# First layers of four gated feed-forwards by a seven-product scheme, with weight sums on GpSimd

## The chip, the cores and the metric

The kernel runs on one core of a Trainium2 chip. The metric is the device time of one execution in microseconds (us). TensorE (PE in the profile) multiplies; VectorE (DVE), ScalarE (ACT) and GpSimd (POOL) work element by element; SyncE (SP) issues the loads.

## What is computed

Two models of width 1024 run one after the other over 512 tokens, all in float32. The first has one block of dilated, stick-breaking and memory attention and a gated feed-forward with a short convolution. The second has two layers, one with a gated block mixer and one with a recurrent mixer (RWKV-7). Each of the two layers has two gated feed-forwards, so there are four of them, called 00, 01, 10 and 11, and they are what is changed:

```python
def swiglu(x, w13, w2):
    gate, up = jnp.split(x @ w13, 2, axis=-1)      # w13: 1024 x 5632, w2: 2816 x 1024
    return (jax.nn.silu(gate) * up) @ w2
```

The input `x` of each is a root-mean-square norm of the residual stream.

## The kernel before

Activations lie transposed in SBUF: a tile is 128 features by 512 tokens, and x has 8 tiles (`KD`). To keep float32's accuracy, every operand of a product is split in a high part (rounded to the fp32r type, a CAST on ScalarE) and a low part (the rest, a subtraction on VectorE), and each product is three matmuls: high by high, high by low, low by high. So `xh`, `xl` are the two parts of x and `wh`, `wl` those of a chunk of weights.

**Weights.** They come in a fixed stream of chunks (`STREAM`, `order`). SyncE loads chunk n into one of two slots of `raw` (128 x 2048, 1 MB) as soon as chunk n-2 has its low part (`lo_ready`). `split_hi` (ScalarE, L320) and `split_lo` (VectorE, L336) split it. `chunks_used` counts the chunks that TensorE has finished.

**The first layer of a feed-forward** is a `linear` stage of 22 units (`KF`), named up_00 and so on. A unit is one chunk: 8 tiles of x by two blocks of 128 output features, one of the gate and one of the value. It issues 8 x 2 x 3 = 48 matmuls (L518) with a moving operand of 128x512, into two banks of PSUM, in turn of two groups of banks. For each unit `swiglu` has VectorE scale both outputs by the norm's factor `rs` (L2443, L2444), ScalarE apply Silu (L2435), VectorE multiply (L2448), ScalarE make the high part `hid_h` (L2424) and VectorE the low part `hid_l` (L2428).

**The norm runs late.** x enters the products with its gain alone; the factor 1/rms is applied to the outputs. `Deferred` (L987) makes `xh` (ScalarE, L1047) and `xl` (VectorE, L1100) tile by tile while the products of units 0 and 1 start. Where a post-norm precedes it, GpSimd adds the tiles to the residual stream (`add_on_pool`, L921). After that, ScalarE squares (L767) and VectorE adds seven times (L859), TensorE sums over partitions (`sum_pe`, L802) inside unit 1, ScalarE takes the root (`square_root`, L776), VectorE inverts and makes a diagonal (L868 to L872), and TensorE spreads it (`spread_pe`, L843) inside unit 2. TensorE stands still wherever one of these is not ready.

**The second layer** (down_00 and so on) has 8 units of two chunks of 1408 columns (`halves`); a unit is 22 tiles by 3 matmuls in one bank. Its first unit waits for each tile of the hidden activations (`norms=Made`, L650), which are all split by then except the last.

Everything is written by hand: each engine has its own list of instructions, with waits on semaphores. An engine never passes a waiting instruction.

## Time and profile before

| | before |
|---|---|
| median of 3 runs | 3256.67 us (3254.47 to 3256.72) |
| profiled execution, first to last instruction | 3256.1 us |
| what lies around it: median less this span | 0.6 us |
| TensorE busy | 3198.5 us (98%), 20322 matmuls |
| VectorE busy | 1772.9 us (54%) |
| ScalarE busy | 1250.6 us (38%) |
| GpSimd busy | 136.1 us (4%), 134 instructions |
| granted TensorE clock | 0.997 of full speed, mean |
| DMA queues | 88 GB/s, 24.7% of 16 engines for the weights |

The profile is one execution. Its page gives busy times, the chain of work that ended last, and groups of instructions; the trace gives single instructions with their start. A row of a matmul shows its whole latency, and the matmuls overlap: the pace is read from the distance of starts.

### The profile page before, as it was taken

The numbers are of one execution on the slowest core, as the hardware profiler recorded it, in microseconds if no ns is written. First come the engines' busy times: TensorE is split into PE (matmuls) and PEld (weight loads), VectorE is DVE, ScalarE is ACT, GpSimd is POOL, SyncE is SP. The second block draws the span as 40 slices with busy tenths as digits, with TensorE's granted clock in tenths as the row PEclk, the third lists the DMA queues.
The fourth block names the chain that finished last, engine by engine and source line by source line (L and its number), as shares of the span: only waits on it lengthen the run. The fifth ranks groups of instructions, "written<-read, shape, count | busy, mean of one in ns | idle before, by whom it ended". The sixth has DMA issues, their size and how long they took to land.

```text
span 3256.1 us, 46645 instructions
## 1 busy us (share of the span) xinstructions
PE 3198.5 (98%) x20322; PEld 2628.9 (81%) x20322; DVE 1772.9 (54%) x2127; ACT 1250.6 (38%) x1605; POOL 136.1 (4%) x134
## 2 busy tenths in 40 slices
PE   9999999999999999999999999999999999999998
PEld 7887787888788888987888887888777777788886
DVE  6456766774454435463644357444666656654437
ACT  3357544443232223442422244223336554332224
POOL 2100000000000001000100011000120000100001
PEclk9999999999999999999999999999999999999999
DMA  5211222222232223222222222222222000232231
GB/s 194 99 53 65 104 91 91 92 103 89 92 104 91 89 96 126 91 78 97 91 99 83 98 99 88 95 95 89 84 80 101 16 4 15 84 104 91 88 106 65
DMA packets 47211, 286.68 MB, mean 88 GB/s; under 512 B 6416, under 2 KB 6688, under 8 KB 21408
## 3 DMA queue, kind: packets, MB, share of 16 engines
q1 hardware_dynamic: 44960, 279.51, 24.7%
q0 software_dynamic: 2048, 4.20, 0.4%
q8 instruction: 160, 2.62, 0.3%
q14 instruction: 43, 0.35, 0.0%
HBM read 277.39 MB, written 2.10 MB: 86 GB/s over the span
## 4 chain that ended last, share of the span: by engine, by line
PE 80%; DVE 5%; ACT 2%; issue 1%; POOL 0%; DVEq 0%; ACTq 0%
PE ps L518 70%; PE ps L3700 3%; PE ps L3738 1%; PE ps L1242 1%; DVE wl L336 1%; ACT wh L320 1%; PE ps L1243 1%; PE ps L1244 1%; DVE xl L3174 0%; PE ps L2790 0%; PE ps L985 0%; DVE tmp L3182 0%; DVE conv L2473 0%; PE ps L3745 0%; PE ps L3777 0%
## 5 line engine op out<-in xcount | busy, mean ns | idle before, releaser
L518 PE MATMUL ps<-xh,wh 128*128 128x512 f32 (+1 forms) x2464 | 966.1, 392 | 13.1 <-DVE xl L3174 3.4
L518 PE MATMUL ps<-xl,wh 128*128 128x512 f32 (+1 forms) x2464 | 941.9, 390 | 3.3 <-POOL xl L3071 3.0
L518 PE MATMUL ps<-xh,wl 128*128 128x512 f32 (+1 forms) x2464 | 910.3, 391 | 0.3 <-DVE wl L336 0.3
L336 DVE TENSOR_TENSOR wl<-raw,wh 128x2048 fp32r<-128x2048 f32 (+2 forms) x283 | 590.4, 2086 | 424.0 <-ACT wh L320 423.7
L320 ACT CAST wh<-raw 128x2048 fp32r<-128x2048 f32 (+1 forms) x280 | 485.9, 1735 | 283.7 <-PE ps L518 275.4
L518 PEld LDWEIGHTS ps<-xh,wh 128*128 128x128 f32 (+1 forms) x2464 | 462.4, 188 | 122.3 <-issue 18.7
L518 PEld LDWEIGHTS ps<-xl,wh 128*128 128x128 f32 (+1 forms) x2464 | 461.7, 188 | 105.1 <-POOL xl L3071 3.8
L518 PEld LDWEIGHTS ps<-xh,wl 128*128 128x128 f32 (+1 forms) x2464 | 461.8, 188 | 99.4 <-issue 1.0
L518 PE MATMUL ps<-hid_h,wh 128*128 128x512 f32 x880 | 342.9, 390 | 1.2 <-DVE wl L336 1.2
L518 PE MATMUL ps<-hid_l,wh 128*128 128x512 f32 x880 | 342.4, 389 | 0.0
L518 PE MATMUL ps<-hid_h,wl 128*128 128x512 f32 x880 | 342.4, 389 | 0.0
L2435 ACT ACTIVATE tmp<-tmp 128x512 f32<-128x512 f32 x88 | 55.8, 634 | 539.4 <-DVE tmp L2443 539.3
L2443 DVE TENSOR_TENSOR tmp<-ps,rs 128x512 f32<-128x512 f32 x88 | 60.8, 691 | 292.7 <-PE ps L518 287.5
L518 PEld LDWEIGHTS ps<-hid_h,wh 128*128 128x128 f32 x880 | 165.2, 188 | 37.0 <-DVE wl L336 3.1
L518 PEld LDWEIGHTS ps<-hid_l,wh 128*128 128x128 f32 x880 | 165.2, 188 | 34.4
L518 PEld LDWEIGHTS ps<-hid_h,wl 128*128 128x128 f32 x880 | 165.2, 188 | 34.2
L921 POOL TENSOR_TENSOR h<-tmp,h 128x512 f32<-128x512 f32 x42 | 66.5, 1612 | 2610.4 <-DVE tmp L914 2610.4
L1293 DVE COPY ybuf<-ps 128x512 f32<-128x512 f32 x40 | 27.7, 692 | 179.6 <-PE ps L518 156.7
L2428 DVE TENSOR_TENSOR hid_l<-tmp,hid_h 128x512 fp32r<-128x512 f32 x110 | 76.2, 693 | 77.1 <-ACT hid_h L2424 77.1
L1337 ACT ACTIVATE tmp<-ybuf 128x512 f32<-128x512 f32 x35 | 22.1, 632 | 246.7 <-DVE ybuf L1293 192.4
L2424 ACT CAST hid_h<-tmp 128x512 fp32r<-128x512 f32 x110 | 68.3, 621 | 86.6 <-DVE tmp L2448 67.0
L518 PE MATMUL ps<-wh,xh 128*128 128x256 f32 x352 | 94.7, 284 | 0.1
(494 smaller groups left out, 4017.7 us busy)
## 6 DMA issues: line engine op xcount, KB each, us to landing
raw<-in_up SPq DMA_DIRECT2D x88, 1024.0 KB, 4.7
raw<-in_down SPq DMA_DIRECT2D x64, 704.0 KB, 4.1
raw<-in_up_c SPq DMA_DIRECT2D x22, 1024.0 KB, 4.7
raw<-in_down_c SPq DMA_DIRECT2D x16, 704.0 KB, 4.0
raw<-in_gates SPq DMA_DIRECT2D x8, 1024.0 KB, 4.7
raw<-in_gv SPq DMA_DIRECT2D x8, 1024.0 KB, 4.8
raw<-in_gu SPq DMA_DIRECT2D x8, 1024.0 KB, 4.7
raw<-in_gout SPq DMA_DIRECT2D x8, 1024.0 KB, 4.7
```

The lines of the kernel that those rows point to most:

```text
L320: nc.scalar.copy(wh[:, slot, 0:w], raw[:, slot, 0:w]).then_inc(hi_ready, 1)
L336: nc.vector.tensor_tensor(wl[:, slot, 0:w], raw[:, slot, 0:w], wh[:, slot, 0:w].bitcast(F32), ALU.subtract).then_inc(lo_ready, 1)
L518: last = nc.tensor.matmul(out, stationary, moving, start=(fresh and q == 0), stop=(t == kt - 1 and half == per - 1 and q == 2), skip_group ...
L921: nc.gpsimd.tensor_tensor(dst, self.scratch(2 + t % 2), dst, ALU.add).then_inc(n_onto.sem, 1)
L1242: nc.tensor.matmul(ps[:, b, :], wh[0:r, slot, wc], hi[0:r], start=(t == 0), stop=False, skip_group_check=True)
L1243: nc.tensor.matmul(ps[:, b, :], wh[0:r, slot, wc], lo[0:r], start=False, stop=False, skip_group_check=True)
L1244: last = nc.tensor.matmul(ps[:, b, :], wl[0:r, slot, wc], hi[0:r], start=False, stop=(t == self.kt - 1), skip_group_check=True)
L2424: nc.scalar.copy(hid_h[:, k, tokens], tmp[:, 2 + u, tokens]).then_inc(act_steps.sem, 1)
L2428: nc.vector.tensor_tensor(hid_l[:, k, tokens], tmp[:, 2 + u, tokens], hid_h[:, k, tokens].bitcast(F32), ALU.subtract).then_inc(dve_steps.s ...
L2435: nc.scalar.activation(tmp[:, u, :], tmp[:, u, :], ACT.Silu).then_inc(act_steps.sem, 1)
L2443: nc.vector.tensor_tensor(tmp[:, u, :], products[0], rs[:, :], ALU.mult).then_inc(dve_steps.sem, 1)
L3700: last = nc.tensor.matmul(out(e, c), left(lhs, e, c), right(rhs, e, c), start=(n == 0), stop=(n == len(pairs) - 1), skip_group_check=True)
```

## The change

Each of the four first layers is now a class of its own, `SwigluUp`, in place of a `linear` stage with `swiglu`.

- Units 0 to 2 (`PLAIN`) are multiplied as before. Units 3 to 21 (19 of 22) go by Strassen's scheme in Winograd's form. The products of a unit form a 2 x 2 block matrix of weights (even or odd tiles of x, gate or value) by a 2 x 2 block matrix of x (even or odd tiles, first or last 256 tokens). Seven block products take the place of eight. Each is 4 pairs of tiles by 3 matmuls with a moving operand of 128x256: 84 matmuls for 48.
- **Terms of x**, once a stage: four combinations for each pair of tiles (`terms`), 16 instructions of 128x256 on VectorE and four on ScalarE, then four CASTs of 128x1024 on ScalarE for their high parts, and their low parts by two subtractions of 128x1024 on VectorE and two on GpSimd.
- **Sums of weights**, for each of the 19 units: GpSimd makes S1 to S4, four instructions of 128x512 (`sums_of`). It starts those of unit u when TensorE has finished unit u-2. Splitting a chunk is now a CAST and a subtraction of 128x1536 (three plain blocks) and two of each of 128x1024 (the sums).
- **Outputs**: ScalarE copies the first product (128x256), VectorE does seven additions of 128x256 that each read one product from PSUM, scales gate and value in one instruction of 128x1024, and multiplies.
- **The split of the hidden activations** is moved out of the units to the end of the stage: 11 CASTs of 128x1024 on ScalarE and 11 subtractions, 8 on VectorE and 3 on GpSimd (`POOL_PAIRS`). The high parts lie where the terms and `xl` were, so the last unit runs pair by pair of tiles to free them.
- The chunks' columns are laid out by quarters, for the convolutional feed-forward too, whose instructions stay as they are. The embedding's split moves from unit 5 of the first layer to unit 2 of the second.

The diff, cut to its core:

```diff
+        def evict(self, dve, unit):
...
+            dve.wait_ge(u_copied.sem, u_copied.after(k, 1))
+            dve.wait_ge(chunks_used, self.a + unit + 3)
+            nc.vector.tensor_tensor(v1, g1, r[5], ALU.add).then_inc(u_added.sem, 1)
...
+        def sums_of(self, pool, unit):
+            n, k, x = self.a + unit, unit - PLAIN, self.slot(unit)
+            pool.wait_ge(raw_ready[n % 2], 16 * (n // 2 + 1))
+            pool.wait_ge(chunks_used, n + 1 if unit > PLAIN else self.a + 3)
...
+            nc.gpsimd.tensor_tensor(s1, a21, a22, ALU.add).then_inc(w_sum.sem, 1)
+            nc.gpsimd.tensor_tensor(s3, a11, a21, ALU.subtract).then_inc(w_sum.sem, 1)
+            pool.wait_ge(chunks_used, n + 1)
+            pool.wait_ge(w_sum.sem, w_sum.after(k, 1))
+            nc.gpsimd.tensor_tensor(s2, s1, a11, ALU.subtract).then_inc(w_sum.sem, 1)
+            pool.wait_ge(w_sum.sem, w_sum.after(k, 3))
+            nc.gpsimd.tensor_tensor(s4, a12, s2, ALU.subtract).then_inc(w_sum.sem, 1)
...
+        def gpsimd(self):
...
+                for j in range(2):
+                    self.term_low(pool, nc.gpsimd, pool_low, j)
+                for unit in range(PLAIN, KF):
+                    self.sums_of(pool, unit)
+                for p in self.POOL_PAIRS:
+                    self.hidden_low(pool, nc.gpsimd, pool_low, p)
...
+        def scalar(self):
...
+                norm.squares_act(act)
+                self.term_high(act, 0)
+                self.term_high(act, 1)
+                n = a + 2
+                split_hi(act, n, 16 * (n // 2 + 1), n % 2, order[n][2])
+                self.term_high(act, 2)
+                self.term_high(act, 3)
+                self.plain_high(act, 3)
+                norm.scale_act(act)
...
+        def vector(self):
...
+                split_lo(dve, a + 1, (a + 1) % 2, order[a + 1][2])
+                self.terms_of(dve, 0)
+                norm.squares_dve(dve)
+                self.terms_of(dve, 2)
+                norm.scale_dve(dve)
+                split_lo(dve, a + 2, a % 2, order[a + 2][2])
...
+                for unit in range(PLAIN, KF - 2):
+                    self.evict(dve, unit)
+                    self.scale(dve, unit)
+                    self.plain_low(dve, unit + 2)
+                    self.hide(dve, unit)
+                    self.sum_low(dve, unit + 2, 0)
+                    self.sum_low(dve, unit + 2, 1)
...
+        def quad_waits(self, pe, unit, i):
+            if i == 0:
+                pe.wait_ge(psum_read.sem, self.read + (1 if unit == PLAIN else unit - 1))
+                pe.wait_ge(w_low.sem, w_low.after(unit - PLAIN, 1))
...
+            if i == 3:
+                pe.wait_ge(w_low.sem, w_low.after(unit - PLAIN, 2))
...
+            if i == 5:
+                pe.wait_ge(lo_ready, self.a + unit + 1)
...
-        linear(f"up_{layer}{n}", KD, 256, x_split, norms=norm, between=between, paired="filled", **swiglu(norm))
-        linear(f"down_{layer}{n}", HALF, P, hid_split, halves=True, norms=Made(lambda t: 4 * t + 4),
-               **(sums or summing(ybuf, 1)))
+        up = SwigluUp(f"up_{layer}{n}", norm)
+        linear(f"down_{layer}{n}", HALF, P, up.split, halves=True, second_ahead=True, norms=up,
+               between=embedding(layer) if embeds else {}, **(sums or summing(ybuf, 1)))
```

How it moves instructions. First VectorE at the start of stage 00, after the last `xl`; before:

```order
L336 TENSOR_TENSOR wl_52<-raw_50,wh_51 128x2048
L859 TENSOR_TENSOR rs_56<-rs_56,tmp_57 128x512 x7
L868 TENSOR_SCALAR stats_59<-ps 128x4
L870 RECIPROCAL stats_59<-stats_59 128x4
L872 TENSOR_TENSOR rs_56<-const_58,stats_59 128x512
```

and with the change:

```order
L344 TENSOR_TENSOR wl_52<-raw_50,wh_51 128x2048
L2722 SCALAR_TENSOR_TENSOR terms_4771<-h_53,vec_49,terms_4771 128x256 x4
L2732 SCALAR_TENSOR_TENSOR terms_4771<-h_53,vec_49,terms_4771 128x256 x2
L2722 SCALAR_TENSOR_TENSOR terms_4771<-h_53,vec_49,terms_4771 128x256 x2
L868 TENSOR_TENSOR rs_56<-rs_56,tmp_57 128x512 x7
L2722 SCALAR_TENSOR_TENSOR terms_4771<-h_53,vec_49,terms_4771 128x256 x4
L2732 SCALAR_TENSOR_TENSOR terms_4771<-h_53,vec_49,terms_4771 128x256 x2
L2722 SCALAR_TENSOR_TENSOR terms_4771<-h_53,vec_49,terms_4771 128x256 x2
L877 TENSOR_SCALAR stats_59<-ps 128x4
L879 RECIPROCAL stats_59<-stats_59 128x4
```

Eight instructions for the terms now stand ahead of the norm's seven adds, and eight between them and the norm's inverse.

VectorE in one unit of the middle of a stage, before:

```order
L336 TENSOR_TENSOR wl_52<-raw_50,wh_51 128x2048
L2443 TENSOR_TENSOR tmp_57<-ps,rs_56 128x512
L2444 TENSOR_TENSOR tmp_57<-ps,rs_56 128x512
L2448 TENSOR_TENSOR tmp_57<-tmp_57 128x512
L2428 TENSOR_TENSOR hid_l_4767<-tmp_57,hid_h_4766 128x512
```

and with the change:

```order
L2695 TENSOR_TENSOR tmp_57<-tmp_57,ps 128x256
L2696 TENSOR_TENSOR tmp_57<-tmp_57,ps 128x256
L2698 TENSOR_TENSOR tmp_57<-tmp_57,ps 128x256
L2700 TENSOR_TENSOR tmp_57<-tmp_57,ps 128x256
L2702 TENSOR_TENSOR tmp_57<-tmp_57,ps 128x256
L2703 TENSOR_TENSOR tmp_57<-tmp_57,ps 128x256
L2705 TENSOR_TENSOR tmp_57<-tmp_57,ps 128x256
L2710 TENSOR_TENSOR tmp_57<-tmp_57,rs_56 128x1024
L2663 TENSOR_TENSOR plain_l_7506<-raw_50,plain_h_7505 128x1536
L2715 TENSOR_TENSOR hid_4768<-tmp_57 128x512
L2673 TENSOR_TENSOR sums_l_7509<-sums_7507,sums_h_7504 128x1024
L2673 TENSOR_TENSOR sums_l_7510<-sums_7508,sums_h_7504 128x1024
```

Five instructions became twelve. GpSimd had none in the units; it now has, at the start of a stage:

```order
L2645 TENSOR_TENSOR terms_l_4772<-terms_4771,terms_h_4770 128x1024 x2
L2635 TENSOR_TENSOR sums_7507<-raw_50 128x512
L2636 TENSOR_TENSOR sums_7507<-raw_50 128x512
L2639 TENSOR_TENSOR sums_7508<-sums_7507,raw_50 128x512
L2641 TENSOR_TENSOR sums_7508<-raw_50,sums_7508 128x512
```

The last four rows stand 19 times in each stage.

## Rows read from the trace of the kernel before

**Rows 1.** The page: busy times, and the chain that ended last by engine and line.

```profile
PE 3198.5 (98%) x20322; PEld 2628.9 (81%) x20322; DVE 1772.9 (54%) x2127; ACT 1250.6 (38%) x1605; POOL 136.1 (4%) x134
...
PE 80%; DVE 5%; ACT 2%; issue 1%; POOL 0%; DVEq 0%; ACTq 0%
```

**Rows 2.** Chain in order of time, stages 00 and 01: start us, us, what.

```profile
906.73 0.79 PE ps L802 x8
...
910.85 0.86 PE ps L843 x2
911.71 335.28 PE ps L518 x1478
...
1276.31 0.79 PE ps L802 x8
...
1280.56 0.86 PE ps L843 x2
```

**Rows 3.** TensorE by time, matmuls of 256 columns: start us, us, engine, line.

```profile
1339.80 0.28 PE L518 MATMUL ps<-wl,xh 128*128 128x256 f32 x1
...
1347.84 0.28 PE L518 MATMUL ps<-wh,xl 128*128 128x256 f32 x1
```

**Rows 4.** VectorE by time, part of one unit of stage 00.

```profile
942.16 0.69 DVE L2443 TENSOR_TENSOR tmp<-ps,rs 128x512 f32<-128x512 f32 x1 [3.94 <-PE ps L518]
942.77 0.68 DVE L2444 TENSOR_TENSOR tmp<-ps,rs 128x512 f32<-128x512 f32 x1
```

**Rows 5.** Busy time in a stretch of stage 00: PE, PEld, DVE, ACT, POOL, clock, DMA share.

```profile
930.00:1120.00 190.00, 190.00 (x840) 157.34 (x839) 87.81 (x90) 54.56 (x55) 0.00 (x0) 1.00 0.27 95
```

**Rows 6.** VectorE: groups by shape with mean ns, and a pair of 256-column instructions.

```profile
L336 DVE TENSOR_TENSOR wl<-raw,wh 128x2048 fp32r<-128x2048 f32 x198 | 455.1, 2298 | 257.8 <-ACT wh L320 257.5 <-DVE vec L1535 0.3
L336 DVE TENSOR_TENSOR wl<-raw,wh 128x1408 fp32r<-128x1408 f32 x80 | 130.0, 1625 | 162.4 <-ACT wh L320 162.4
...
3236.69 0.76 DVE L2614 TENSOR_TENSOR tmp<-ps,rs 128x256 f32<-128x256 f32 x2 [2.73 <-PE ps L518]
```

**Rows 7.** GpSimd and VectorE by time while both work, before stage 01.

```profile
1253.35 1.28 POOL L921 TENSOR_TENSOR h<-tmp,h 128x512 f32<-128x512 f32 x1 [1127.40 <-DVE tmp L914]
...
1253.46 1.72 DVE L1100 SCALAR_TENSOR_TENSOR xl<-h,vec,xh 128x512 fp32r<-128x512 f32 x1 [0.20 <-ACT xh L1047]
...
1259.38 0.73 DVE L914 SCALAR_TENSOR_TENSOR tmp<-ybuf,vec,ps 128x512 f32<-128x512 f32 x1
1260.04 1.13 DVE L1100 SCALAR_TENSOR_TENSOR xl<-h,vec,xh 128x512 fp32r<-128x512 f32 x1
1261.09 0.74 DVE L914 SCALAR_TENSOR_TENSOR tmp<-ybuf,vec,ps 128x512 f32<-128x512 f32 x1
...
1266.59 0.75 DVE L1100 SCALAR_TENSOR_TENSOR xl<-h,vec,xh 128x512 fp32r<-128x512 f32 x1 [0.30 <-ACT xh L1047]
```

**Rows 8.** The same two engines at the recurrent mixer's start, and one GpSimd line's durations.

```profile
2369.15 3.12 DVE L336 TENSOR_TENSOR wl<-raw,wh 128x2048 fp32r<-128x2048 f32 x1
...
2370.08 3.08 POOL L3124 TENSOR_TENSOR dx<-hn 128x511 f32<-128x511 f32 x1
...
L3124 POOL TENSOR_TENSOR dx<-hn x8: 1034/1487/3084, 2367.2 to 2379.2; 128x511 f32<-128x511 f32 x8
```

**Rows 9.** VectorE and ScalarE by time at the start of stages 00 and 01.

```profile
896.75 5.46 DVE L859 TENSOR_TENSOR rs<-rs,tmp 128x512 f32<-128x512 f32 x7
...
908.20 0.69 DVE L872 TENSOR_TENSOR rs<-const,stats 128x512 f32<-128x512 f32 x1
...
1269.46 5.46 DVE L859 TENSOR_TENSOR rs<-rs,tmp 128x512 f32<-128x512 f32 x7
...
903.64 1.91 ACT L320 CAST wh<-raw 128x2048 fp32r<-128x2048 f32 x1 [2.36 <-PE ps L518]
915.88 0.62 ACT L2424 CAST hid_h<-tmp 128x512 fp32r<-128x512 f32 x1 [0.76 <-DVE tmp L2448]
```

**Rows 10.** The page: issues of the chunks of the first layers, KB each, us to landing.

```profile
raw<-in_up SPq DMA_DIRECT2D x88, 1024.0 KB, 4.7
```

399 lines of the change are left out of this document (370 added, 29 removed).

## The prediction

> **What bounds the kernel now.** I read the page first: TensorE is busy for 98% of the span and is 80% of the chain that ended last [rows 1]; the granted clock is 1.00 of full speed, 2.4 GHz, in the stretch used below [rows 5]. Then the chain in order of time: in stage 00, 1478 matmuls follow one another for 335.28 us without a wait, through the rest of the first layer and the second [rows 2]. That is 226.8 ns for one with 512 columns. So only what shortens TensorE's list, or makes it wait, counts; before the change there is no stall at the seam between the layers. Last, busy time in a stretch of the same stage: VectorE works 87.8 of 190 us, ScalarE 54.6, GpSimd not at all [rows 5]. A unit takes 48 x 226.8 ns = 10.89 us, and VectorE has half of it free. The chunk for a unit lands 4.7 us after its issue [rows 10] and is not late in any case below.
>
> **1. TensorE's products.** Matmuls with 256 columns start 120 ns apart: 67 of them lie in the 8.04 us from 1339.80 to 1347.84 [rows 3]. A seven-product unit is 84 x 120 ns = 10.08 us, 0.81 less than 10.89. Over 19 units and four stages that is 61 us saved. The rows are of products with x stationary, here the weights are; the load of the stationary operand has the same form, so I take 120 ns. From 129.6 ns up the gain would be gone (10.89 / 84). The Trainium skill, "TensorE: Matmul & The Clock Gate", section "Back-to-back issue gap", gives N/2.4 + 2.5 ns for a single warm matmul, 109 and 216 ns; by it a unit would gain 1.2 us, this term would be 91 us instead of 61, and the case below in which TensorE sets the pace would end 30 us earlier. The rows here show 120 and 227 ns, so I keep the rows.
>
> **2. VectorE's turn per unit.** Instructions of 512 columns start 0.61 us apart [rows 4]; the two L336 shapes give (2298 - 1625) / 640 = 1.05 ns a column; two of 256 take 0.76 us, so they start 0.34 apart [rows 6]. Hence 1024 columns take 1.15 us and 1536 take 1.68. A turn is seven PSUM additions (7 x 0.34, and some 0.3 for results awaited), scale 1.15, low part of the plain blocks 1.68, multiply 0.61, low parts of the sums 2 x 1.15: 8.4 us. Alone it would fit in 10.08.
>
> **3. But it is not alone: GpSimd.** A sum of 512 columns takes it 1.28 us, and while it runs, a VectorE instruction with two inputs in SBUF stands: L1100 at 1253.46, begun 0.11 us after GpSimd's, takes 1.72 us instead of the 0.75 of the one at 1266.59 [rows 7]. L914, which has one input in PSUM, takes its usual 0.73 beside it. In the steady alternation L914 recurs after 1.71 us, of which VectorE's 512 columns are 0.53, so GpSimd keeps it out for 1.17 [rows 7]. It goes both ways: a GpSimd instruction whose shortest is 1.03 us took 3.08 when it met L336, and L336 took 3.12 instead of 2.30 [rows 8, 6]. When both want the way, they alternate; back-to-back VectorE instructions do not keep GpSimd out (L336 at 2369.15 was let in last). The Trainium skill, "SBUF — State Buffer", section "Who interferes with whom", says that a VectorE instruction with two SBUF inputs contends with a GpSimd instruction that reads SBUF, and that whoever issues first keeps the other out for the whole instruction. By that the hold would be 1.28, the turn worked out below 12.2 us, and the sum 53 us higher. The rows agree on who waits, and show 1.17.
>
> For the sums I take 1.12: the nearest row is L921 (1.17), but S1 and S3 read both inputs from one tile, as L3124 does, whose shortest is 1.03 (a hold of some 0.93) [rows 8]. The ends are 0.93 and 1.28. The seven PSUM additions (2.7 us) are free ground for two sums. The other two each hold VectorE: 8.4 + 2 x 1.12 = 10.6 us, over TensorE's 10.08. So VectorE falls behind by half a microsecond or more a unit. TensorE does not feel it at first: unit u+2 starts on the low part of the plain blocks, which VectorE has after 2.7 + 1.15 + 2.2 (holds) + 1.68 = 7.7 us of its turn, 2.3 us in hand. But GpSimd is released by TensorE's end of a unit, not by VectorE; once VectorE is late, the sums fall on the low-part subtractions of the turn before and only one lies beside the additions. Then three are paid: 8.4 + 3 x 1.12 = 11.8 us; I take 11.7. With five of the 19 units at 10.08 and 14 at 11.7: 14 x 1.62 = 22.7 us a stage, **+91 us** in all. Ends: nothing (hold 0.93 to 1.08, never late), and 17 x 2.1 = 36 us a stage (hold 1.28, late at once).
>
> **4. The start of a stage.** In 00, VectorE began its seven adds at 896.75 and took 5.46 [rows 9]. Eight term instructions (0.40 each, 0.34 and a scalar operand's 0.06) go ahead: adds end at 905.4, before TensorE's sum at 906.73 [rows 2]. In 01 the adds end at 1269.46 + 3.2 + 5.5 = 1278.1, and the sum was at 1276.31: 1.8 us late. Then eight more term instructions, 3.2 us alone, with both inputs in SBUF. Beside them GpSimd now has two low parts of 1024 columns (twice 1.17, estimate 2.3 each) and four sums, 9 us, and each can hold one short term instruction: +8 (0 to 9), so they end at 905.4 + 11.2 = 916.6. ScalarE stands behind them with two CASTs of 1024 columns and one of 1536 ahead of the root. From 0.62 and 1.91 us for 512 and 2048 columns [rows 9] the last of these and the root add 2.5: 919.1. Inverse and diagonal about 1 (the diagonal alone 0.69 [rows 9]), spread 0.86 [rows 2]: 921.0 for 911.71, **9.3 us**. In 01 the adds end 3.0 us later relative to the spread (1278.1 against 1280.56, 905.4 against 910.85): 12.3. The other two stages have a post-norm too, I count them as 01. Sum 9.3 + 3 x 12.3 = **+46 us**. Without any hold the term instructions would end at 908.6, the three CASTs and the root at 912.1 and the spread at 914.0, 2.3 us late, and 5.3 in the others: 18, since the CASTs ahead of the root remain. That is the low end; with 9 us of holds the high end is 50.
>
> **5. The seam.** The hidden activations are split at the end. After the products of unit 20 VectorE has: additions and scale 3.9, split of a chunk 1.6 (1408 columns [rows 6]), five low parts 5.8, another chunk 1.6, additions and scale of unit 21 3.9, two low parts and two multiplies 3.5, a wait for ScalarE's last CAST 1.0 and the last low part 1.2: 22.5 us. GpSimd's three low parts of 1024 columns hold it for up to 6.9 more: 29. TensorE wants the last pair 10.08 + 15.0 - 1.4 = 23.7 us after unit 20. So it waits 5 to 8 (VectorE starts late, by 3): I take 7.5, **+30 us** in all; bounds 2 (no hold) and 9 a stage. The rest of the second layer has little VectorE work, the embedding's split, moved there, is hidden by it, and would cost its few microseconds if it were not. The x tiles' copies by quarters change addresses alone: 0.
>
> **Sum**, against the execution profiled (3256.1, 0.6 under the median): -61 + 91 + 46 + 30 = +106 us, or 3363 with the 0.6.
>
> **Rivals.**
> - *Units stay at TensorE's pace.* Start and seam are held as above, but the sums are short like L3124 and VectorE never falls behind (decides: hold under 1.08 us). -61 + 46 + 4 x 6.5 = +11: 3268. For it: two of four sums have both inputs in one tile. Against: L921 at 1253.35, with nothing in its way, took 1.28 [rows 7]; and L3124's inputs lie one element apart, which the sums' don't.
> - *Faster: the holds hardly bite.* GpSimd is released just when VectorE begins its additions from PSUM, which rows show undelayed; if GpSimd then runs beside additions and ScalarE's waits only, TensorE sets the pace, with 18 us for the starts and 8 for the seams: -61 + 18 + 8 = -35: 3222. It decides where fewer than two sums a unit and none of the term instructions are held. Against it: the rows show a hold at every meeting.
> - *The half-width products don't run at 120 ns.* At 135 ns a unit is 11.3 us: +34 us from TensorE instead of -61; beside a VectorE at 11.7 it adds nothing, beside a free one it gives about 3257 + 34 + 26 = 3317.
>
> **How the numbers follow.** Forecast 0.60, units at TensorE's pace 0.18, faster 0.17, slow products 0.05. Time 3363. The range reaches down to the faster case, 3218, and up to 3390, which takes in a hold of 1.17 (11.9 us a turn, 15 units late, +17 us) and 10 us more at starts and seams; a hold of 1.28 (3416) and the best of the faster cases are left out, some 0.15 together. A run of this kernel can tell 0.2%, 6.5 us. The faster case and the short end of the second make 0.20 for faster; 3268 with its bounds gives 0.07 within 0.2%; the rest, 0.73, is slower. The likeliest case's own range is 3335 to 3390.
>
> **What would show it.** Right: GpSimd's L2635 to L2641 well over 1.28 us each; VectorE's L2663 and L2673 at a mean over 0.6 us above 1.76 and 1.22; TensorE's ends of units 10.1 us apart at first and 11.7 later, idle in front of the first product of a unit, released by VectorE's L2663; a wait of 9 us or more at L843; one of some 7 us in the second layer's first unit. Wrong: 84 matmuls every 10.1 us to the end of a stage, or GpSimd's sums at 1.0 us, or a short wait at L843.

## The result, and the profile after

| | before | after |
|---|---|---|
| median | 3256.3 us (4 runs) | 3326.2 us (3319.9 to 3329.8, 4 runs) |
| ratio | | 1.0212 [1.0198, 1.0227] |
| profiled execution, span | 3256.1 us | 3328.0 us |
| TensorE, VectorE, GpSimd busy | 98%, 54%, 4% | 96%, 69%, 22% |
| mean granted clock | 0.997 | 0.986 |

Slower by 70 us (2.1%), where 106 were forecast. The execution that was profiled is the slowest of the four and lies 3.6 us above their median, so the profile accounts for 71.9 us and not 70. The page of the changed kernel, which answers to [rows 1]:

```profile
PE 3179.5 (96%) x23058; PEld 2724.9 (82%) x23058; DVE 2303.2 (69%) x2739; ACT 1401.7 (42%) x1821; POOL 723.7 (22%) x458
```

TensorE has less to do and waits more. The way to see where the time went is one instruction that stands once at the head of every stage: VectorE's reciprocal of the norm after the previous part. In the following lines "the reciprocal" is always this one. Its rows, of the kernel before and then of the changed one:

```profile
881.81 0.95 DVE L864 RECIPROCAL rs<-rs 128x128 f32<-128x128 f32 x1 [1.85 <-ACT rs L772]
1248.97 0.95 DVE L864 RECIPROCAL rs<-rs 128x128 f32<-128x128 f32 x1 [0.58 <-ACT rs L772]
1539.53 0.95 DVE L864 RECIPROCAL rs<-rs 128x128 f32<-128x128 f32 x1 [0.58 <-ACT rs L772]
1908.70 0.95 DVE L864 RECIPROCAL rs<-rs 128x128 f32<-128x128 f32 x1 [1.16 <-ACT rs L772]
```

```profile
882.43 0.95 DVE L873 RECIPROCAL rs<-rs 128x128 f32<-128x128 f32 x1 [1.85 <-ACT rs L781]
1271.06 0.95 DVE L873 RECIPROCAL rs<-rs 128x128 f32<-128x128 f32 x1 [0.58 <-ACT rs L781]
1561.60 0.95 DVE L873 RECIPROCAL rs<-rs 128x128 f32<-128x128 f32 x1 [0.58 <-ACT rs L781]
1946.37 0.95 DVE L873 RECIPROCAL rs<-rs 128x128 f32<-128x128 f32 x1 [1.16 <-ACT rs L781]
```

Stage 00 is the first interval, the mixer between is the second, stage 01 the third: 367.16 and 388.63 us; 290.56 and 290.54; 369.17 and 384.77. Read in the same way, stage 10 went from 369.95 to 386.23 and 11 from 369.49 to 385.60. So 21.5, 15.6, 16.3 and 16.1 us, 69.5 of the 71.9 by which the spans differ, and nothing elsewhere but 2.4. Inside a stage there are three places, and TensorE's idle time shows them. Start of stages 00 and 01:

```profile
921.56 2.08 PE L852 MATMUL ps<-rs,const 128*128 128x512 f32 x2 [10.10 <-DVE rs L881]
...
1606.26 2.08 PE L852 MATMUL ps<-rs,const 128*128 128x512 f32 x2 [8.05 <-DVE rs L881]
```

Then the units by halves (3 to 21, whose products are 256 tokens wide): TensorE's wait in front of a unit's first product is 0.21 us in stage 01, but 1.3 in the second half of stage 00.

```profile
1059.32 0.36 PE L2825 MATMUL ps<-xh,plain_h 128*128 128x256 f32 x1 [1.30 <-DVE plain_l L2663]
1070.93 0.36 PE L2825 MATMUL ps<-xh,plain_h 128*128 128x256 f32 x1 [1.31 <-DVE plain_l L2663]
...
1709.06 0.36 PE L2825 MATMUL ps<-xh,plain_h 128*128 128x256 f32 x1 [0.21 <-DVE plain_l L2663]
1719.58 0.35 PE L2825 MATMUL ps<-xh,plain_h 128*128 128x256 f32 x1 [0.21 <-DVE plain_l L2663]
```

A unit takes 11.61 us in stage 00 and 10.52 in stage 01. TensorE's units are not late at once: in each stage the first seven by halves start 10.08 us apart. And the seam between the two layers, six waits of 6.9 us together in stage 01 (five are shown):

```profile
1819.83 0.50 PE L527 MATMUL ps<-terms_h,wh 128*128 128x512 f32 x1 [0.69 <-DVE hid_r L2533]
...
1825.86 0.50 PE L527 MATMUL ps<-xl,wh 128*128 128x512 f32 x1 [1.71 <-DVE wl L344]
1830.76 0.50 PE L527 MATMUL ps<-xl,wh 128*128 128x512 f32 x1 [1.23 <-DVE hid_r L2533]
1835.45 0.50 PE L527 MATMUL ps<-terms_l,wh 128*128 128x512 f32 x1 [1.29 <-DVE last_hid_r L2533]
1838.79 0.47 PE L527 MATMUL ps<-terms_h,wh 128*128 128x512 f32 x1 [1.67 <-DVE wl L344]
```

Added up by TensorE's starts against the reciprocal: starts +13.0, +16.2, +16.9 and +17.1 (63), lateness in the units 14 and three times 5 (29), seams 9.7 each (39), elsewhere 2.4, and -61.4 for products of 120 ns. That is 72. Of each seam's 9.7 us some 2.3 are handed on by the late units: with no unit late, in runs 1 and 4, the rest of a stage behind the start of its last unit is shorter by that. Late units therefore cost 29 + 4 x 2.3, some 38 us in all.

**Why two rhythms.** One turn of VectorE and GpSimd in stage 01, and one in stage 00:

```profile
1728.20 1.75 DVE L2663 TENSOR_TENSOR plain_l<-raw,plain_h 128x1536 fp32r<-128x1536 f32 x1
1729.87 0.69 DVE L2715 TENSOR_TENSOR hid<-tmp 128x512 f32<-128x512 f32 x1
1730.47 4.56 DVE L2673 TENSOR_TENSOR sums_l<-sums,sums_h 128x1024 fp32r<-128x1024 f32 x2
...
1730.03 1.68 POOL L2635 TENSOR_TENSOR sums<-raw 128x512 f32<-128x512 f32 x1 [3.00 <-PE ps L2827]
1731.67 2.27 POOL L2636 TENSOR_TENSOR sums<-raw 128x512 f32<-128x512 f32 x1
1733.90 2.28 POOL L2639 TENSOR_TENSOR sums<-sums,raw 128x512 f32<-128x512 f32 x1
1736.26 1.30 POOL L2641 TENSOR_TENSOR sums<-raw,sums 128x512 f32<-128x512 f32 x1
...
1092.24 1.75 DVE L2663 TENSOR_TENSOR plain_l<-raw,plain_h 128x1536 fp32r<-128x1536 f32 x1
1093.91 1.78 DVE L2715 TENSOR_TENSOR hid<-tmp 128x512 f32<-128x512 f32 x1
1095.62 4.54 DVE L2673 TENSOR_TENSOR sums_l<-sums,sums_h 128x1024 fp32r<-128x1024 f32 x2
...
1093.44 1.71 POOL L2635 TENSOR_TENSOR sums<-raw 128x512 f32<-128x512 f32 x1 [3.72 <-DMA raw<-in_up]
1095.11 1.75 POOL L2636 TENSOR_TENSOR sums<-raw 128x512 f32<-128x512 f32 x1
```

The pair L2673 alone takes 2.35 us, L2715 0.68. When a VectorE instruction has to stand while one of GpSimd's runs, I call that a hold. A hold costs VectorE (4.56 - 2.35) / 2 = 1.10 us. In these rows the two engines alternate, one of GpSimd's sums to one of VectorE's instructions: what counts is not how many sums there are but how many VectorE instructions with both inputs in SBUF stand between the first sum and the additions from PSUM. In stage 01 the sums begin just behind the start of L2715 and hold two; in stage 00 they begin while L2663 still runs, hold three, and the turn is 1.1 us longer. In stage 00 they are released by the chunk's landing, 5 us after VectorE's turn began and its load was issued; in 01 by TensorE's end of a unit, 5.6 us after. Each rhythm keeps itself up, as these rows suggest: what releases the sums is itself timed by VectorE's or TensorE's last turn.

### The profile page after: what moved, and what is told of

It reads as the page before. It is cut to its first block and busy times, and to the rows that moved or that the text cites. A ratio compares the mean times of both kernels' runs of the same rounds, so it can differ in the third digit from the quotient of the medians.

```text
span 3328.0 us, 53477 instructions
## 1 busy us (share of the span) xinstructions
PE 3179.5 (96%) x23058; PEld 2724.9 (82%) x23058; DVE 2303.2 (69%) x2739; ACT 1401.7 (42%) x1821; POOL 723.7 (22%) x458
## 5 line engine op out<-in xcount | busy, mean ns | idle before, releaser
L344 DVE TENSOR_TENSOR wl<-raw,wh 128x2048 fp32r<-128x2048 f32 (+1 forms) x207 | 415.9, 2009 | 330.6 <-ACT wh L328 330.3
L527 PE MATMUL ps<-xl,wh 128*128 128x512 f32 x1248 | 479.9, 392 | 14.5 <-DVE wl L344 7.7
L328 ACT CAST wh<-raw 128x2048 fp32r<-128x2048 f32 (+2 forms) x204 | 340.9, 1671 | 273.5 <-PE ps L527 264.7
L527 PE MATMUL ps<-xh,wh 128*128 128x512 f32 x1056 | 416.2, 394 | 14.5 <-DVE xl L1109 4.0
L527 PE MATMUL ps<-xh,wl 128*128 128x512 f32 x1056 | 390.1, 392 | 0.3 <-DVE wl L344 0.3
L527 PEld LDWEIGHTS ps<-xl,wh 128*128 128x128 f32 x1248 | 233.4, 187 | 69.5 <-DVE wl L344 9.9
L2673 DVE TENSOR_TENSOR sums_l<-sums,sums_h 128x1024 fp32r<-128x1024 f32 x152 | 285.1, 1910 | 0.1
L2825 PE MATMUL ps<-terms_h,sums_h 128*128 128x256 f32 x912 | 259.3, 284 | 2.0 <-DVE sums_l L2673 2.0
L2826 PE MATMUL ps<-terms_l,sums_h 128*128 128x256 f32 x912 | 258.5, 283 | 0.0
L2827 PE MATMUL ps<-terms_h,sums_l 128*128 128x256 f32 x912 | 258.5, 283 | 0.0
L527 PE MATMUL ps<-hid_r,wh 128*128 128x512 f32 x640 | 250.8, 392 | 0.0
```

Source lines behind the costliest of these rows:

```text
L328: nc.scalar.copy(wh[:, slot, 0:w], raw[:, slot, 0:w]).then_inc(hi_ready, 1)
L344: nc.vector.tensor_tensor(wl[:, slot, 0:w], raw[:, slot, 0:w], wh[:, slot, 0:w].bitcast(F32), ALU.subtract).then_inc(lo_ready, 1)
L527: last = nc.tensor.matmul(out, stationary, moving, start=(fresh and q == 0), stop=(t == kt - 1 and half == per - 1 and q == 2), skip_group ...
L2673: nc.vector.tensor_tensor(x.sums_l[part][:, :, :], x.sums[part][:, :, :], x.sums_h[:, 2 * part:2 * part + 2, :].bitcast(F32), ALU.subtract ...
L2825: nc.tensor.matmul(out, high, moving, start=(j == 0 and i % 2 == 0), stop=False, skip_group_check=True)
L2826: nc.tensor.matmul(out, high, moving_low, start=False, stop=False, skip_group_check=True)
```

## The experiments

Each ran on the chip beside the kernel before, whose median was 3255.8 to 3257.0 us, so 1 or 2 us between two runs say nothing. Gains are against the changed kernel's 3326.2. Lengths of single stages are read from the reciprocal's rows of one profiled execution each.

**1. No weight sums.**

```
-            nc.gpsimd.tensor_tensor(s1, a21, a22, ALU.add)
+            nc.gpsimd.tensor_tensor(s1[:, 0:1], a21[:, 0:1], a22[:, 0:1], ALU.add)
```

and so for s3, s2 and s4; sum_high and sum_low read the raw quarters instead of the sums. So this kernel leaves out the sums of the weights.

> GpSimd's four instructions of a weight sum are cut from 512 columns to 1, and ScalarE and VectorE split the raw quarters in place of the sums, with instructions of the same size; so this kernel leaves out the summing of the weights. Theory A (a GpSimd sum keeps a VectorE instruction with two SBUF inputs waiting about 1.10 us; three stages pay two holds a unit and run at 10.51 us, stage 00 pays three and runs at 11.6): without sums every unit of all four stages takes 10.08 us, the second-half splits take 1.22 us each in place of a mean of 1.91, the 29 us of late units vanish, and each start loses four holds of 1.1 us ahead of VectorE's root work, another 18 us at most: 3326 - 29 - 18 = 3279, between 3275 and 3297. Theory B (VectorE's own list of 8.4 us and ScalarE's order make the units late, the holds fall into VectorE's free time): the pace of the units stays at 10.5 and 11.6 us, only the starts gain: 3308 to 3326.

Measured: 3274.0 us, 52 less. VectorE's group of the sums' splits:

```profile
L2677 DVE TENSOR_TENSOR sums_l<-raw,sums_h 128x1024 fp32r<-128x1024 f32 x152 | 179.2, 1219 | 0.0
```

In the changed kernel its mean was 1910 ns. VectorE's first additions stand 10.08 us apart in all four stages from the second unit by halves to the last but one, so theory A holds for the units. By the stages' lengths that is worth 37 us, with what late units hand on to the seam. The starts got 4 us shorter each (stage 01's first unit by halves ends 62.1 us after the reciprocal in place of 66.4), and keep some 9 to 13 us which are not the sums' doing. Theory B falls: VectorE's own list fits.

**2. TensorE kept busy while it waits.**

```
                     if n == 5:
+                        for _ in range(16):
+                            nc.tensor.matmul(ps[:, 3, 0:2 * P], table("ident"), const[:, 0:2 * P], start=True, stop=True)
                         norm.spread_pe(pe)
```

> TensorE computes 16 matmuls of 128x256 on a constant in the stretch in which it waits for the scale ahead of the spread (L852), and is idle there no more. Theory C (beside the 8 to 10 us of the wait, each start pays for matmuls at half the clock behind it: the spread took 2.08 us where it took 0.86 before): the wait's end stays, the granted clock behind it stays near full, the spread takes 0.86 us again and each start gains 3 us: 3326 - 12 = 3314, between 3308 and 3319. Rival D (the clock's drop falls where TensorE would wait for VectorE anyway, or the starts' 62 us are all wait): no change, 3324 to 3328. If the 16 matmuls outlast the wait, each start loses what sticks out, up to 2 us a stage: 3334.

Measured: 3316.6 us, 9.6 less, near what theory C gave, but mostly not for its reason. The granted clock (the number behind the five engines' busy times) around the wait in stage 00, changed kernel and this one:

```profile
911.00:921.00 10.00, 0.46 (x3) 0.03 (x1) 6.90 (x9) 3.47 (x4) 5.70 (x5) 0.63 0.00 0
921.00:935.00 14.00, 13.44 (x50) 10.43 (x51) 13.28 (x12) 5.83 (x7) 0.86 (x1) 0.78 0.31 94
```

```profile
911.00:921.00 10.00, 6.77 (x31) 5.55 (x30) 6.89 (x9) 3.47 (x4) 4.73 (x4) 1.00 0.00 0
921.00:935.00 14.00, 14.00 (x81) 12.12 (x80) 14.00 (x11) 7.20 (x8) 4.49 (x3) 1.00 0.29 92
...
920.58 1.13 PE L852 MATMUL ps<-rs,const 128*128 128x512 f32 x2 [3.23 <-DVE rs L881]
```

In the changed kernel the clock is 0.50 of full speed, 1.2 GHz, in every 2 us from 915 to 927, so for 6 us of products too. That drop goes, and the spread takes 1.13 us in place of 2.08. TensorE's first product by halves starts 2.6 us earlier in stage 00, 1.7 in 01, 2.5 and 2.6 in 10 and 11, which is the clock's price at the start. But VectorE, which then sets the pace, takes part of it back: that unit's products are added up only 2.2 us earlier in stage 00, 1.0 in 01, 1.8 in 11, and stages 01, 10 and 11 end up 0.9, 1.5 and 1.7 us shorter. Stage 00 is 9.3 shorter, since with another phase it fell out of its slow rhythm: its last units take 10.52 us. So the clock costs 1.7 to 2.6 us where it is low and 1 to 2 us at the end of a stage, not 3, and that the total agrees is luck. (The stages' gains add up to more than 9.6, because this run's profiled execution is its fastest and the changed kernel's its slowest.) A total alone would have confirmed the wrong price.

**3. Squares and root first, the terms' low halves on VectorE.**

VectorE, then ScalarE; GpSimd's two term_low go, and VectorE takes all four.

```
                 split_lo(dve, a + 1, (a + 1) % 2, order[a + 1][2])
-                self.terms_of(dve, 0)
                 norm.squares_dve(dve)
-                self.terms_of(dve, 2)
+                self.terms_of(dve, 0)
                 norm.scale_dve(dve)
                 split_lo(dve, a + 2, a % 2, order[a + 2][2])
-                for j in (2, 3):
-                    self.term_low(dve, nc.vector, t_made, j)
+                self.terms_of(dve, 2)
                 self.plain_low(dve, 3)
-                self.sum_low(dve, 3, 0)
                 self.evict_plain(dve, 0)
+                for j in range(KPAIRS):
+                    self.term_low(dve, nc.vector, t_made, j)
+                self.sum_low(dve, 3, 0)
...
                 norm.squares_act(act)
-                self.term_high(act, 0)
-                self.term_high(act, 1)
                 n = a + 2
                 split_hi(act, n, 16 * (n // 2 + 1), n % 2, order[n][2])
-                self.term_high(act, 2)
-                self.term_high(act, 3)
-                self.plain_high(act, 3)
-                norm.scale_act(act)
+                norm.two.square_root(act)
+                self.term_high(act, 0)
+                self.term_high(act, 1)
+                self.plain_high(act, 3)
+                norm.keep_scale(act)
+                self.term_high(act, 2)
+                self.term_high(act, 3)
```

> At the start of each of the four stages the sums of squares come first on VectorE and ScalarE, the first two term pairs next, then the root, and the other two pairs behind it; the low halves of all four terms are taken on VectorE, none on GpSimd. Nothing is left out. Theory A: GpSimd's two low halves (2.5 us each undisturbed) held VectorE's terms for 5 us; with them gone and the root ahead, the wait for the scale at L852 falls from 8.05 and 10.10 us to under 2, the clock stays up, and what is left is lateness of the first unit by halves, which waits for the low halves of the terms, 3 to 6 us a stage: 3326 - 4 x 10 = 3286, between 3276 and 3298. Rival E (the start is bound by the sum of VectorE's work before the first product on halves, not by its order): the wait moves whole from L852 to the first unit by halves, and only the saved holds show, 4 x 2 us: 3318.

Measured: 3294.4 us, 32 less. The wait at L852 is gone in stage 00, and fell only to some 4 us in the other three, not under 2. A further wait, for VectorE to take unit 2 out of PSUM (L2686), took over 2.51 us of it in stage 01; stage 01's first unit by halves ends 59.8 us after the reciprocal (66.4):

```profile
1581.00 2.08 PE L852 MATMUL ps<-rs,const 128*128 128x512 f32 x2 [4.08 <-DVE rs L881]
...
1601.63 0.39 PE L2824 MATMUL ps<-terms_h,sums_h 128*128 128x256 f32 x1 [2.51 <-DVE tmp L2686]
```

6.6, 5.8 and 7.3 us came in stages 01, 10 and 11, and 16.1 in 00, of which 9.5 again are its rhythm. Rival E's 8 us in all is too little. But order and holds were changed in one run, which doesn't part them. What is left of the wait is what GpSimd's four sums, begun at 1571.99, cost the terms: the four term instructions beside them take 5.77 us, the four at 1583.07 take 1.67. Run 7, which starts the sums later, has no such wait.

**4. The scale read from PSUM.**

```
-            nc.vector.tensor_tensor(self.both(unit), self.both(unit), self.spread_scale(), ALU.mult)
+            for b, half in ((3, SOON), (7, LATER)):
+                x = self.both(unit)[:, :, half]
+                nc.vector.tensor_tensor(x, x, ps[:, b, T // 2:T].unsqueeze(1).broadcast_to([P, 2, T // 2]), ALU.mult)
```

ScalarE copies rs there once a stage, behind open(2). The upper halves of these two banks are free, but TensorE writes the other half of such a bank in a unit's seventh product, so it waits there until the scale of the unit before is done.

> The scale of the tokens is copied by ScalarE into two free half banks of PSUM once a stage, and the multiplication of a unit's gate and value by it reads it there, as two instructions of 2x256 columns in place of one of 2x512 that reads SBUF twice; the last two units stay as they were. Nothing is left out. Theory A (only instructions with both inputs in SBUF are held): the instruction that meets the first sum is held no more, VectorE's turn ends inside 10.08 us and most of the 29 us of late units vanish: 3326 - 25 = 3301, between 3295 and 3308. Rival F (the two instructions are longer than one and the next one with two SBUF inputs is held in its place, so the turn stays at 10.5 us): 3322 to 3332.

Measured: 3289.4 us, 37 less. All units of all stages take 10.08 us on average, as without any sums; since the sums are all made here, it was not ScalarE's waiting for them that run 1 took away. Groups of this run's instructions say why:

```profile
L2720 DVE TENSOR_TENSOR tmp<-tmp,ps 128x512 f32<-128x512 f32 x136 | 87.5, 685 | 7.0
L2725 DVE TENSOR_TENSOR hid<-tmp 128x512 f32<-128x512 f32 x80 | 130.1, 1626 | 0.1
L2676 DVE TENSOR_TENSOR sums_l<-sums,sums_h 128x1024 fp32r<-128x1024 f32 x152 | 183.4, 1241 | 0.2
```

With one input in PSUM the scale is never held (685 ns, 512 columns). Three sums pass beside it and the additions, and the fourth, which itself stands while VectorE splits the plain blocks, holds L2725 (1626 ns in place of 685): one hold a unit. VectorE is then faster than TensorE and stays ahead. The Trainium skill, "SBUF — State Buffer", section "Who interferes with whom", says that a VectorE instruction with at most one SBUF input, outside the modes that take two ports, does not contend with GpSimd; these rows agree. The forecast of 25 us was 12 short: it took most of the 29 us of TensorE's late starts, and not the 2.3 us a stage that late units hand on to the seam. Stage 00 is 16.2 us shorter, the others 6 to 8. Rival F falls.

**5 and 6. The seam.** First only the three low halves moved from GpSimd to VectorE:

```
-        POOL_PAIRS = (1, 4, 7)
+        POOL_PAIRS = ()
```

> The three low halves of hidden pairs 1, 4 and 7 that GpSimd takes at the seam of the two layers go to VectorE, in the order of the pairs; nothing else is moved. Theory A (GpSimd's and VectorE's low halves hold each other: VectorE's took 2.69, 3.43 and 3.43 us where an undisturbed one takes 1.21, GpSimd's 8.9 us for three): VectorE does all of them in 1.14 us apiece, is done earlier by 2.69+3.43+3.43-3x1.21 less 3x1.14 = 2.5 us, the second chunk's split and all behind it come 2.5 us earlier, and each seam of 9.7 us gains 1.7 (the 1.71 wait for that split) and up to 1 more of the later waits: 3326 - 4 x 2.2 = 3317. Rival G (the seam's waits come from ScalarE's order, which splits the second chunk behind nine high halves): under 0.5 us a stage, 3324 to 3327.

Measured: 3313.0 us, 13 less; stage 01 is 3.5 us shorter. On VectorE the instructions of L2533, which took 1.23, 2.69, 3.43 and 3.43 us in a row, are now (the group of one form), and TensorE's waits in stage 01's seam are these three alone:

```profile
L2533 DVE TENSOR_TENSOR hid_r<-hid,xl 128x1024 fp32r<-128x1024 f32 x12 | 14.6, 1219 | 0.0
...
1825.20 0.50 PE L527 MATMUL ps<-xl,wh 128*128 128x512 f32 x1 [1.17 <-DVE hid_r L2533]
1829.88 0.50 PE L527 MATMUL ps<-terms_l,wh 128*128 128x512 f32 x1 [1.27 <-DVE last_hid_r L2533]
1833.22 0.47 PE L527 MATMUL ps<-terms_h,wh 128*128 128x512 f32 x1 [1.68 <-DVE wl L344]
```

More than forecast: holds cost more than GpSimd's help was worth. The waits of 0.69, 0.33 and 1.71 us are gone; the last of these was for the second chunk's split, so it was the holds and not ScalarE's order that made that split late. Rival G falls. Then also the order:

ScalarE's part, then VectorE's, where low half 6 to 9 move likewise:

```
-            split_hi(act, n, 16 * (n // 2 + 1), n % 2, order[n][2])
             self.copy_first(act, KF - 1)
-            self.hidden_high(act, HALF - 2)
+            split_hi(act, n, 16 * (n // 2 + 1), n % 2, order[n][2])
+            for p in range(6, HALF - 1):
+                self.hidden_high(act, p)
             self.open(act, KF - 1)
...
-            self.hidden_low(dve, nc.vector, s_low, 6)
             split_lo(dve, n, n % 2, order[n][2])
+            self.hidden_low(dve, nc.vector, s_low, 6)
             self.evict(dve, KF - 1)
             self.scale(dve, KF - 1)
-            self.hidden_low(dve, nc.vector, s_low, 8)
             self.hide(dve, KF - 2)
-            self.hidden_low(dve, nc.vector, s_low, 9)
+            self.hidden_low(dve, nc.vector, s_low, 7)
+            self.hidden_low(dve, nc.vector, s_low, 8)
             self.hide(dve, KF - 1)
+            self.hidden_low(dve, nc.vector, s_low, 9)
```

> As the run with all low halves on VectorE, and the order at the seam changed: ScalarE copies the last unit's first product and splits the second chunk before high halves 6 to 9, VectorE takes that chunk's split before low half 6 and combines the last unit's products before low halves 7 to 10. Theory A with G (both the holds and the order cost): of the waits at the seam (0.69, 0.33, 1.71, 1.23, 1.29 and 1.67 us, 6.9 together) all but about 1.5 go: 3326 - 4 x 5.2 = 3305, between 3300 and 3312. Rival H (the waits hang on the last unit's chain of sums, scale, activation, product and splits, some 7 us behind TensorE's end, whatever the order): 3316 as the run before.

Measured: 3308.1 us, 18 less, so the order gave 5 beyond the holds; under half of the 12 it was to give. Some 5 us a seam are left. Rival H, which put the whole seam down to the last unit's chain, goes too far, since the order gave something. 1.7 of the 5 us are the split of the second layer's third chunk, as run 9 shows; whether H explains the others was not tried.

**7. All together.** Runs 3, 4 and 6 in one, and in addition:

```
+                self.norm.wait_columns(pool)
                 for unit in range(PLAIN, KF):
+                    if unit == PLAIN + 1:
+                        pool.wait_ge(psum_read.sem, self.read + PLAIN)
                     self.sums_of(pool, unit)
...
                 self.hide(dve, 0)
+                self.evict_plain(dve, 2)
                 self.sum_low(dve, 3, 1)
                 self.hide(dve, 1)
-                self.evict_plain(dve, 2)
```

> All changes in one kernel that computes the reference: squares and root first, low halves of the terms on VectorE, GpSimd's first sums only once the reciprocal is there and the second ones once unit 2 is out of PSUM, unit 2 taken out before the last splits of unit 3's weights; the scale read from PSUM; and the seam's new order. Theory A: start 3294 - 3326 = -32 by the run with the root first, and about 5 us a stage more, since the 4.08 us wait at L852 and the half clock behind it go: -50; scale from PSUM -37 (as measured alone); seam -20: 3326 - 107 = 3219, between 3205 and 3235, and so faster than the kernel before at 3256. Rival (the parts overlap: a start that ends earlier finds VectorE's list longer in the first units, and what the seam gains was slack of the late units): 3245 to 3260.

Measured: 3251.6 us (11 runs), ratio to the kernel before 0.9983 [0.9974, 0.9992]: faster by 0.2%, but 33 us over the forecast and outside its range. By the stages of the profiled execution the late units gave their 37 us and the seams 17 of 20, so the miss lies in the starts: 22 of 50. Of the missing 28, 9.5 are stage 00's slow rhythm, which both run 3 and run 4 had removed and which was counted twice. For the rest, L852's wait did vanish, but VectorE's list then bound the first units by halves, and a wait of my own came behind it:

```profile
1581.38 0.39 PE L2839 MATMUL ps<-xh,plain_h 128*128 128x256 f32 x1 [2.57 <-DVE tmp L2693]
...
1596.19 0.39 PE L2839 MATMUL ps<-xh,sums_h 128*128 128x256 f32 x1 [3.00 <-ACT ps L2611]
```

The second is the copy of the scale into PSUM, queued on ScalarE behind a high half that waits for GpSimd.

**8. The sums' phase alone.**

```
                 for unit in range(PLAIN, KF):
+                    if unit >= PLAIN + 2:
+                        pool.wait_ge(u_added.sem, u_added.after(unit - 2 - PLAIN, 6))
                     self.sums_of(pool, unit)
```

> GpSimd's sums for unit u+2 wait until VectorE has added up unit u's products (3 us behind TensorE's end of unit u, which released them before); nothing else is moved. Theory A with the rhythm (a unit pays a hold of 1.1 us for each sum that finds VectorE at an instruction with two SBUF inputs; with the early start two of the four sums pass beside the seven additions that read PSUM): three or four holds a unit now in all four stages, a period of 11.6 us or over in place of 10.51: stages 01, 10 and 11 lose 17 units x 1.1 us each, 56 together, stage 00 some 8: 3326 + 64 = 3390, between 3370 and 3460 (with four holds). Rival (the period of 11.6 us in stage 00 comes from the load of its weights, which landed late there, and not from where the sums fall): stages 01 to 11 stay at 10.51 us, 3326 to 3335.

Measured: 3454.3 us, near the upper end. Every unit of every stage takes 12.5 us, four holds: scale, L2665, L2717 and a split of sums. The same work on every engine, moved by some microseconds, costs 128 us. The rival, by which stage 00 alone was slow through its late load of weights, would have left the other stages at 10.51 us. One turn:

```profile
1035.97 2.02 DVE L2712 TENSOR_TENSOR tmp<-tmp,rs 128x1024 f32<-128x1024 f32 x1
1037.92 2.83 DVE L2665 TENSOR_TENSOR plain_l<-raw,plain_h 128x1536 fp32r<-128x1536 f32 x1
1040.78 1.66 DVE L2717 TENSOR_TENSOR hid<-tmp 128x512 f32<-128x512 f32 x1
1042.36 2.29 DVE L2675 TENSOR_TENSOR sums_l<-sums,sums_h 128x1024 fp32r<-128x1024 f32 x1
...
1035.62 1.29 POOL L2635 TENSOR_TENSOR sums<-raw 128x512 f32<-128x512 f32 x1 [4.53 <-DVE tmp L2705]
```

**9. All, with the two waits mended.** The first is the copy, which leaves its old place, the second the wait for the split of the second layer's third chunk, whose low part VectorE takes behind its last low half.

```
                 self.open(act, 1)
+                act.wait_ge(psum_read.sem, self.read + PLAIN)
+                for b, half in ((3, SOON), (7, LATER)):
+                    nc.scalar.copy(ps[:, b, T // 2:T], rs[:, half]).then_inc(t_start.sem, 1)
...
             self.open(act, KF - 1)
+            n = self.a + KF + 2
+            split_hi(act, n, 16 * (n // 2 + 1), n % 2, order[n][2])
             self.hidden_high(act, HALF - 1)
```

> As the run with all changes, with two things mended: ScalarE copies the scale into PSUM right behind unit 2's way out of PSUM and no longer behind unit 4's first sums (TensorE waited 3.0 and 3.3 us for that copy), and the split of the second layer's third chunk comes ahead of ScalarE's last high half (TensorE waited 1.5 us). Theory: both waits go, 4 x 4.7 = 19 us: 3252 - 19 = 3233, between 3230 and 3242; 0.7% under the kernel before. Rival (VectorE is so late with the first units' splits that the wait only moves to the next product): 3244 to 3252.

Measured: 3255.6 us, between 3249.0 and 3269.7 in 12 runs; a miss: it is above both ranges. The second edit did what it should: the seam is 1.7 us shorter than in run 7 in stages 00, 10 and 11. The first did harm: up to the first unit's additions VectorE is as early as in run 7 (63.4 us after the reciprocal in both, in stage 01), but there its next two turns were 8.35 and 9.66 us, and here they are 10.57. The wait of 3.0 us had held TensorE back long enough for VectorE to be ahead. Without it the sums, released by TensorE, fall beside VectorE's splits, and stage 01 of the profiled run kept a period of 10.57 us to its end (376.1 us), while stages 00 and 11 caught up to 10.08 after ten and five units. That other stages do so in the slower executions would explain the spread, but only one execution has a trace, so it is not shown.

**10 and 11. The sums kept in step.**

```
+                    if unit >= PLAIN + 2:
+                        pool.wait_ge(lo_ready, self.a + unit)
                     self.sums_of(pool, unit)
```

> The kernel with all changes mended, and one wait more: from the sums of the third unit by halves on, GpSimd's sums for unit u+2 wait until VectorE has split the weights of unit u+1, so that they always start beside the seven additions of unit u that read PSUM (in the run before, stage 01 ran at 10.57 us a unit because they were released by TensorE in the middle of VectorE's splits and held two of them; where VectorE was ahead it was one hold and 10.08). Theory: one hold a unit in all stages, VectorE's turn of about 9.7 us catches up 0.4 us a unit, every stage settles at 10.08 us, and the runs lie close together again: 3255.6 less some 8 us for stage 01 in the profiled run, less what the mended waits give: 3236, between 3230 and 3244. Rival (the later sums come too late for ScalarE's high halves, and TensorE waits for the sums' splits in their place): 3250 to 3275.

Measured: 3233.4 us (3231.6 to 3233.8), ratio to the kernel before 0.9929 [0.9916, 0.9943]. VectorE's turns are 9.48 us until it has caught up with TensorE after seven units, then 10.08 in all stages: one wait more, 22 us less, and a spread of 2 us in 5 runs in place of 21 in 12. Stages 00 and 01 take 359.6 and 363.8 us (before: 367.2 and 369.2). One turn:

```profile
1102.11 1.29 DVE L2731 TENSOR_TENSOR tmp<-tmp,ps 128x512 f32<-128x512 f32 x2
...
1099.54 1.30 POOL L2646 TENSOR_TENSOR sums<-raw 128x512 f32<-128x512 f32 x1 [3.40 <-PE ps L2851]
...
1103.45 2.76 POOL L2652 TENSOR_TENSOR sums<-raw,sums 128x512 f32<-128x512 f32 x1
```

The wait alone, on the changed kernel:

> The changed kernel with that wait alone. The sums start with the seven additions (2.9 us of 5.2), the scale that follows reads SBUF twice and is held, and one more: two holds a unit in every stage. Theory: stage 00 goes from 11.6 to 10.51 us for its last nine units, the other stages stay: 3326 - 9 = 3317, between 3312 and 3321. Rival (the wait itself delays the sums and with them the splits): 3326 and over.

Measured: 3321.7 us; stage 00 fell from 388.6 to 379.7 us, at 10.51 us a unit, and the others grew by 0.3 to 1. The theory's 10.51 us came true; the total is 0.7 us above its range (3312 to 3321) and below the rival's.

## Why the prediction was right, and where its sizes were off

- **Direction and mechanism.** Slower was forecast with 0.73, because the sums on GpSimd hold VectorE, the root comes late and the hidden splits stand at the seam. All three were found. The rivals are out: units did not stay at TensorE's pace, the holds bit, and the half-width products do run at 120 ns (10.08 us a unit in run 1). The term of -61 stands. By an estimate with the formula of the Trainium skill, "TensorE: Matmul & The Clock Gate", section "Back-to-back issue gap", for a single matmul, it would have been -91. This case's trace does not agree: no unit took less than 10.08 us where TensorE set the pace.
- **Luck.** 3326 lies inside the stated range, 3218 to 3390, since that reaches down to the faster case, but under the likeliest case's own, 3335 to 3390. And it is no further off only because errors of opposite sign cancelled in part: the units were put 62 us too high, the rest 28 too low. With the measured 29 in the units' place the forecast would have been 3301. In that term the rival with the units at TensorE's pace, which had 0, was nearer than the forecast with 91.
- **The signs.** GpSimd's sums (1.6 to 1.9 us on average), L2673 (1.91) and the seam's waits (6.9) came as the forecast said. L2663 did not (2.03 on average, not over 2.36), the units at 11.7 us came in stage 00 alone, and so did the spread's wait of 9 us or more (10.10; about 8 in the others).
- **The hold** (step 3): 1.12 was taken, 1.10 measured; a hold for the whole 1.28 us is further off. The Trainium skill, "SBUF — State Buffer", section "Who interferes with whom", has the other engine kept out for the whole instruction; the rows agree on who waits, and not on the length.
- **Units** (step 3), +91: 29 was measured. This is the step that failed. It said that once VectorE is late "only one lies beside the additions. Then three are paid". Holds were counted by sums; they go by VectorE's instructions met, since the two engines alternate. With the sums behind L2715 only the two L2673 are left, so two are paid, 8.3 + 2 x 1.10 = 10.5 us. Only stage 00 paid three, at 11.61 us, near the 11.7 taken; and there only in units 13 to 20. The lateness also reached TensorE after seven units and not after five.
- **Start** (step 4), +46: 63. For 00 the step gave a spread 9.3 us late. It began 10.25 late (921.56 against 910.69 in the rows below, less 0.62 for the reciprocals). What came on top was the clock, which no term held: spread 2.08 us for 1.02, and slow products behind it, 1.7 to 2.6 us up to the first product by halves by run 2. For 01 the rows were the wrong ones: those of [rows 2, 9] from 1269 to 1281 us, and [rows 7], belong to the mixer between the stages, which has the same norm; as examples of a hold the latter serve as well. Stage 01's own spread began 30.3 us after its reciprocal and not 31.4, so the 12.3 should have been 13.4. It began 14.4 us late. The three rows of the kernel before, of stage 00, the mixer and stage 01:

```profile
910.69 1.02 PE L843 MATMUL ps<-rs,const 128*128 128x512 f32 x2
...
1280.39 1.02 PE L843 MATMUL ps<-rs,const 128*128 128x512 f32 x2
...
1569.83 1.02 PE L843 MATMUL ps<-rs,const 128*128 128x512 f32 x2
```

- **Seam** (step 5), 7.5 a stage: 9.7. VectorE's lateness was put at 3 and is 2.3; the held low parts were 3.5 (run 5). What the step did not see is the split of the second layer's third chunk, behind ScalarE's last high half: a wait of 1.67 us, gone with run 9's edit.
- Together: +17 at the starts, +9 at the seams, +2 elsewhere, -62 in the units make the 34 us between the forecast's 106 and the profile's 72.

What stays open: what of the start's 9 to 13 us without sums is VectorE's work and what its order; why stage 00 alone fell into the slow rhythm in all of the changed kernel's profile (that it depends on the phase is shown by runs 2, 3, 8 and 11, what sets the phase is argued).

## What to carry to other kernels

When GpSimd helps VectorE out of the same memory, do not count what is moved but what is held: each VectorE instruction with both inputs in SBUF that meets a GpSimd one pays most of that one's length (1.10 of 1.28 us here). Start the helper where the other engine reads PSUM, and tie that start with a wait to that place in its program, since a loop that only follows buffers coming free settled here in rhythms of 10.5 or 11.6 us by its phase alone. And when gains of single edits are added up, look where each was made: two that both break the same bad rhythm count once.

## What the chip showed that was not expected

- The same instructions on the same engines ran at 10.5, 11.6 or 12.5 us a unit, and stayed there for eight units or more, by the phase of one engine against another alone (the changed kernel and run 8); with the scale read from PSUM it was 10.08 or 10.57 (run 9).
- Taking a wait of 3 us away, together with one of 1.5 at the seam, raised a kernel's median by 4 us and spread its runs over 21 us (run 9); adding one took 22 us off (run 10).
- During and after a wait of 10 us TensorE's granted clock fell from 2.4 to 1.2 GHz (0.63 and 0.78 of full speed as means of two stretches, rows of run 2), yet its own cost was small beside the wait: 1.7 to 2.6 us at the start, 1 to 2 at the end of a stage.
